# Eighteen more projection slices as seven products of halves in a hybrid mixer and MoE layer

## The reference

```python
proj = x @ w_in                       # 1024 -> 8 groups: lru_x, lru_y, ml_q, ml_k, ml_v, ml_o, gd_q, gd_k, gd_v, gd_z, gates
ha = rg_lru(causal_conv(lru_x), ...) * gelu(lru_y)                    # branch a
hb = rms_norm(mlstm_chunkwise(ml_q, ml_k, ml_v, ...)) * sigmoid(ml_o) # branch b
qkv = silu(causal_conv(concat(gd_q, gd_k, gd_v)))
hc = rms_norm(gated_delta_chunked(l2(q), l2(k), v, g, beta)) * silu(gd_z)  # branch c
merged = sum(sigmoid(gates[n]) * (h[n] @ w_br[n]) for n in range(3))
x = layer_norm(ALPHA * x + merged @ w_out)
x = layer_norm(ALPHA * x + moe(x))    # 32 experts, top 4, SwiGLU, d_ff 1024
```

## Time and profile before

| | us |
|---|---|
| median of three runs | 1292.63 (1292.39 to 1293.22) |
| profiled execution, its own time | 1292.72 |
| its span, first to last instruction | 1290.9 |
| PE busy in the span | 1247.0 (97%) |
| DVE busy | 375.3 (29%) |
| ACT busy | 163.7 (13%) |
| POOL busy | 103.3 (8%) |
| bytes moved | 463.06 MB, mean 359 GB/s |

### The profile page before, as it was taken

The page is one execution under the profiler, slowest core; times in us unless marked ns, Lnnn a source line. Parts: engine busy times, 40 slices in busy tenths (PEclk is TensorE's granted clock), DMA queues, the critical chain, the costliest instruction groups (busy, mean ns, idle before and its releaser), DMA issues.

```text
span 1290.9 us, 18843 instructions
## 1 busy us (share of the span) xinstructions
PE 1247.0 (97%) x8098; PEld 684.6 (53%) x8098; DVE 375.3 (29%) x821; ACT 163.7 (13%) x283; POOL 103.3 (8%) x89
## 2 busy tenths in 40 slices
PE   9999999999999999999999999999899999999896
PEld 8888889999864344344343443434243333434342
DVE  4857583553443120211202112121111112120213
ACT  1441621121030000000000000000000000000001
POOL 1000035644100000000000000000000000000001
PEclk9999999999999999999999999999999999999999
DMA  7645227357899999999999999999999999999995
GB/s 271 204 136 181 102 99 293 123 216 289 327 368 423 421 429 409 427 426 427 427 414 428 427 428 425 428 427 427 426 428 429 425 430 428 428 426 429 428 428 238
DMA packets 51180, 463.06 MB, mean 359 GB/s; under 512 B 11896, under 2 KB 13840, under 8 KB 17072
## 3 DMA queue, kind: packets, MB, share of 16 engines
q1 hardware_dynamic: 45280, 459.85, 86.6%
q10 hardware_dynamic: 5840, 2.32, 0.7%
HBM read 460.68 MB, written 1.47 MB: 358 GB/s over the span
## 4 chain that ended last, share of the span: by engine, by line
PE 68%; DMA 20%; issue 1%; POOL 0%; DVE 0%; ACT 0%; POOLq 0%; SPq 0%; DVEq 0%
PE ps L1164 26%; DMA mix<-expert_w 10%; PE ps L1182 10%; DMA ring<-expert_w 10%; PE ps L684 7%; PE ps L1061 4%; PE ps L1073 4%; PE ps L707 4%; PE ps L1157 3%; PE ps L984 2%; PE ps L718 1%; PE ps L1173 1%; PE ps L808 1%; PE ps L1191 1%; PE ps L937 0%
## 5 line engine op out<-in xcount | busy, mean ns | idle before, releaser
L1164 PE MATMUL ps<-ring,mix 128*64 128x512 f32 x1512 | 338.3, 592 | 0.1
L1164 PEld LDWEIGHTS ps<-ring,mix 128*64 128x64 f32 x1512 | 106.5, 137 | 194.8 <-issue 190.6
L1182 PE MATMUL ps<-ring,mix 128*64 128x512 f32 x752 | 170.1, 594 | 19.5 <-DMA ring<-expert_w 19.5
L707 PE MATMUL ps<-mix 128*128 128x256 f32 x736 | 162.1, 380 | 0.0
L707 PEld LDWEIGHTS ps<-mix 128*128 128x128 f32 x736 | 138.7, 190 | 19.7 <-issue 1.2
L2176 DVE TENSOR_SCALAR mix<-ps 128x512 f32<-128x512 f32 x32 | 22.1, 692 | 370.6 <-PE ps L1164 370.6
L1164 PE MATMUL ps<-mix 128*64 128x512 f32 x536 | 121.1, 593 | 3.9 <-DMA mix<-expert_w 3.7
L1182 PEld LDWEIGHTS ps<-ring,mix 128*64 128x64 f32 x752 | 53.0, 137 | 120.5 <-issue 98.0
L2185 DVE COPY mix<-ps 128x512 f32<-128x512 f32 x32 | 22.1, 692 | 240.6 <-PE ps L1173 240.6
L647 POOL TENSOR_TENSOR mix<-mix 128x1024 f32<-128x1024 f32 (+1 forms) x2 | 3.4, 1700 | 955.9 <-ACT mix L1592 955.9
L1164 PEld LDWEIGHTS ps<-mix 128*64 128x64 f32 x536 | 37.6, 137 | 77.0 <-issue 69.8
(11 more groups left out here) (294 smaller groups left out, 940.1 us busy)
## 6 DMA issues: line engine op xcount, KB each, us to landing
ring<-expert_w SPq DMA_DIRECT2D x121, 2048.0 KB, 30.7
mix<-expert_w SPq DMA_DIRECT2D x39, 2048.0 KB, 29.7
mix<-stream_w SPq DMA_DIRECT2D x42, 1024.0 KB, 4.9
ring<-expert_w SPq DMA_DIRECT2D x41, 1024.0 KB, 10.0
mix<-expert_w SPq DMA_DIRECT2D x22, 1024.0 KB, 21.8
mix<-stream_w SPq DMA_DIRECT2D x8, 512.0 KB, 4.2
mix<-first_w SPq DMA_DIRECT2D x4, 512.0 KB, 4.9
mix<-planes ACTq DMA_DIRECT2D x1, 1024.0 KB, 7.2
```

Source lines behind the costliest of these rows:

```text
L707: ins = mm(o[:, m * S:(m + 1) * S], w[:, c, m * P:(m + 1) * P], XT[c] if rhs is None else rhs[:, c, :], start=(m == 0 and c == 0), stop=(c ...
L1164: ins = mm(PS[64 * a:64 * a + 64, bank + g, :], XE[j][:, c, 64 * a:64 * a + 64], w[a][:, g * 512:g * 512 + 512], start=False, stop=(c == K ...
L1182: ins = mm(PS[64 * a:64 * a + 64, bank + h, :], HT[:, c // 4, c % 4, 64 * a:64 * a + 64], w[a][:, h * 512:h * 512 + 512], start=(c == 0), ...
```

## The change

`halved` now also holds for gz0, gz1 and for a new class `early`: lx, ly, mq, mk, mv, mo and gq2, gq3, which is 18 slices more. Each takes two PSUM banks. For gz, the result is put together by ACT and DVE as for the gates. For the 16 early slices it is put together by ACT and POOL: ACT copies the first bank into the slice's own tile and the second bank into one of two buffers `PB3` (`both_parts`), which waits for the finish of the slice two before; POOL's `finish` adds the pieces with eight additions of 128 columns and increments `combined`, and whoever read the slice waits for that. POOL's order is written out: sums run two slices ahead of the finish. For mv0 and mv1, which need tokens on the partitions, the operands of each product are exchanged. The sums of the branch input move from POOL to DVE (`branch_sums`). mo's sigmoid becomes an operation of its own behind the finish. DVE does `conv_lru(0)` behind the heads. The homes of `HAS` and `WS` move, so that expert place 5 is loaded earlier (after ga11) and the tail piece later.

```diff
 def halved(name):
-    return name[:2] == "ga" or name[:3] == "br0"
+    return name[:2] in ("ga", "gz") or name[:3] == "br0" or early(name)
+def early(name):
+    return name[:2] in ("lx", "ly", "mq", "mk", "mv", "mo") or name in ("gq2", "gq3")
...
-        HAS = [area(MIX, 112 + 2 * n, 512).rearrange("p (c n) -> p c n", n=P) for n in range(4)]
+        HAS = [area(RING, 88 + 2 * n, 512).rearrange("p (c n) -> p c n", n=P) for n in range(4)]
+        WS = [[area(MIX, 111 + 6 * k + 2 * n, 512).rearrange("p (c n) -> p c n", n=P) for n in range(3)] for k in range(2)]
+        PB3 = [area(MIX, 123 + 1.5 * n, 384).rearrange("p (q n) -> p q n", n=P) for n in range(2)]
+        PSUMS = area(MIX, 126, P)
...
                 if name == "ga11":
                     full(sp, closing("br03"))
-                    sp.dma_start(TAIL, expert_w[...]).then_inc(E("tail_in"), 16)
+                    sp.wait_ge(E("state"), NC)
+                    load_steps(5, 0, 5)
...
             full(sp, closing("ga23"))
-            load_steps(5, 0, 5)
+            sp.dma_start(TAIL, expert_w[...]).then_inc(E("tail_in"), 16)
...
+            def finish(name, dst):
+                i = early_at[name]
+                moved(gp, name + "a")
+                moved(gp, name + "b")
+                corners, middle = dst
+                b = PB3[i % 2]
+                nc_g.tensor_tensor(PSUMS, middle[0], middle[1], ALU.add)
+                nc_g.tensor_tensor(corners[1], corners[0], corners[1], ALU.add).then_inc(E("pool_own"), 1)
+                gp.wait_ge(E("pool_own"), 3 * i + 1)
+                for v in middle:
+                    ins = nc_g.tensor_tensor(v, v, corners[1], ALU.add)
+                ins.then_inc(E("pool_own"), 1)
+                gp.wait_ge(E("pool_own"), 3 * i + 2)
+                nc_g.tensor_tensor(corners[1], corners[1], PSUMS, ALU.add)
+                nc_g.tensor_tensor(corners[0], corners[0], b[:, 0, :], ALU.add)
+                for n, v in enumerate(middle):
+                    ins = nc_g.tensor_tensor(v, v, b[:, 1 + n, :], ALU.add)
+                ins.then_inc(E("pool_own"), 1)
+                gp.wait_ge(E("pool_own"), 3 * i + 3)
+                gp.sem_inc(E("combined"), 1)
...
+            weight_sums(at("gq2"))
+            weight_sums(at("gq3"))
+            finish("gq2", quarters(GIN[:, :, 3:], 2))
+            finish("gq3", quarters(GIN[:, :, 3:], 3))
+            weight_sums(at("lx0"))
+            weight_sums(at("lx1"))
+            for n in range(4):
+                weight_sums(at(f"lx{n + 2}" if n < 2 else f"ly{n - 2}"))
+                finish(f"lx{n}", quarters(LX[:, :, 3:], n))
             gp.wait_ge(E("gsilu_v"), 1)
             clear(X_, 0.0)
             clear(XTi, 0.0)
+            for n in range(4):
+                weight_sums(at(f"ly{n + 2}" if n < 2 else ("mq", "mk")[n - 2]))
+                finish(f"ly{n}", quarters(LY, n))
+            finish("mq", quarters(QM, 0))
+            weight_sums(at("mv0"))
+            finish("mk", quarters(MK, 0))
+            weight_sums(at("mv1"))
...
-            gp.wait_ge(E("ha_ready"), 1)
-            moving_sums(4, HAS, ...)
-            gp.wait_ge(E("mss"), 2 * NT)
-            for i in range(len(in_halves)):
+            for n in range(2):
+                weight_sums(at(f"mo{n}"))
+                finish(f"mv{n}", by_token(n))
+            for n in range(2):
+                weight_sums(at(f"gz{n}"))
+                finish(f"mo{n}", quarters(MO, n))
+            for i in range(at("ga00"), len(in_halves)):
                 weight_sums(i)
...
                     if made:
                         pe.wait_ge(E("weight_sums"), 4 * i + made)
+                    if name[:2] == "mv":
+                        lhs, rhs = rhs, lhs
...
+            def both_parts(name, dst, scale=1.0):
+                i = early_at[name]
+                full(act, name + "a")
...
+                nc_s.mul(dst, src, scale).then_inc(free(name + "a"), 1)
+                if i >= 2:
+                    act.wait_ge(E("combined"), i - 1)
+                full(act, name + "b")
+                nc_s.mul(PB3[i % 2].rearrange("p q n -> p (q n)"), ps(name + "b")[:, 0:3 * P], scale
+                         ).then_inc(free(name + "b"), 1)
...
             for n in range(6):
-                moved(dve, f"gq{n}")
+                if f"gq{n}" in early_at:
+                    dve.wait_ge(E("combined"), early_at[f"gq{n}"] + 1)
+                else:
+                    moved(dve, f"gq{n}")
...
             def gelu_argument():
-                for n in range(4):
-                    moved(dve, f"ly{n}")
+                dve.wait_ge(E("combined"), early_at["ly3"] + 1)
...
+            def branch_sums():
+                b11, b12, b21, b22 = [LY[:, 4 * k:4 * k + 4, t * P:(t + 1) * P] for k in range(2) for t in range(NT)]
+                for n, (dst, left, right) in enumerate(((HAS[0], b12, b11), (HAS[1], b22, HAS[0]), (HAS[2], b22, b12),
+                                                        (HAS[3], b21, HAS[1]))):
+                    tt(dst, left, right, ALU.subtract).then_inc(E("moving_sums"), 1)
+                    dve.wait_ge(E("moving_sums"), 4 + n + 1)
```

More of the change, by code:

```diff
@@ L234, in layer_kernel @@
     in_halves = [name for name, _, _ in stream if halved(name)]
+    early_at = {name: n for n, name in enumerate(name for name in in_halves if early(name))}
+    late_at = {name: n for n, name in enumerate(name for name in in_halves if not early(name))}
     def stream_value(n):
@@ L709, in proj @@
                                  start=(m == 0 and c == 0), stop=(c == nk - 1), skip_group_check=True)
[L710 to L719, removed]
                 done(name, ins)
@@ L826, in fill @@
                         if name == "ms00":
[L827 to L828 removed]
+                            pe.wait_ge(E("combined"), early_at["mk"] + 1)
                         t = int(name[3])
@@ L841, in fill @@
                         pe.wait_ge(E("ms_ready"), 1)
-                        for n in range(2):
-                            moved(pe, f"mv{n}")
+                        pe.wait_ge(E("combined"), early_at["mv1"] + 1)
                         for t in range(NT):
@@ L1437, in evac_v @@
             def evac_v(n):
-                full(act, f"mv{n}")
-                nc_s.copy(V1[:, :, 2 * n:2 * n + 2, 0:128],
-                          ps(f"mv{n}").rearrange("p (t h e) -> p t h e", t=NT, h=2)).then_inc(free(f"mv{n}"), 1)
+                both_parts(f"mv{n}", V1[:, :, 2 * n:2 * n + 2, 0:P].rearrange("p t h e -> p h t e"))
             act.wait_ge(E("gelu"), 2)
@@ L1450, in _ @@
             A(LU, LU, ACT.Sqrt).then_inc(E("lu"), 1)
-            evac("mo0", MO[:, 0:2, :], func=ACT.Sigmoid)
+            evac("mo0", MO[:, 0:2, :])
             for t in range(NT):
@@ L1460, in _ @@
                   scale=1.0 / MV).then_inc(E("mss"), 1)
-            evac("mo1", MO[:, 2:4, :], func=ACT.Sigmoid)
+            evac("mo1", MO[:, 2:4, :])
             for n in range(2):
[L1464 to L1467, removed]
+                act.wait_ge(E("combined"), early_at[f"mo{n}"] + 1)
+                A(MO[:, 2 * n:2 * n + 2, :], MO[:, 2 * n:2 * n + 2, :], ACT.Sigmoid).then_inc(E("zsig"), 1)
             def first_part(name, dst):
@@ L1472, in first_part @@
                 nc_s.copy(dst, ps(name + "a")).then_inc(E("part_copied"), 1)
+            for n in range(2):
+                first_part(f"gz{n}", GZ[:, 2 * n:2 * n + 2, :].rearrange("p c s -> p (c s)"))
+                moved(act, f"gz{n}b")
+                A(MT[n], GZ[:, 2 * n:2 * n + 2, :].rearrange("p c s -> p (c s)"), ACT.Sigmoid).then_inc(E("zsig"), 1)
+            gates = [f"{n}{d}" for kind, n, d in branch_items() if kind == "ga"]
             def gate(k):
@@ L1851, in mlstm_gate @@
             def mlstm_gate():
-                for n in range(2):
-                    moved(dve, f"mo{n}")
+                dve.wait_ge(E("zsig"), 2)
                 for h in range(MH):
@@ L1973, in o_gate @@
             def o_gate(t):
-                for n in range(2):
-                    moved(dve, f"gz{n}")
                 full(dve, f"ot{t}")
```

63 lines of the change are left out of this document (34 added, 29 removed).

## The result

The changed kernel takes 1362.83 us (median of 4 runs, 1361.23 to 1364.82), the kernel before 1292.93 (1292.39 to 1293.46): a ratio of 1.0541, 95% interval 1.0523 to 1.0560, or **+69.9 us**. The direction was forecast, the size was not: the sum said +34.3, and the result lies beyond the range. The profiled execution is the slowest of the four, 1364.82; its span is 1363.0.

What follows compares the result with a forecast made beforehand. PE's own work was taken to bound the first stage, full DMA engines the second, shifting as a block. Scores 38.3 us late less 4.0 given back made +34.3 on 1292.72, 1327.0; range 1297 to 1345.

Steps and rivals of the forecast that it cites:

- the sum: Whole kernel: scores 38.3 us late, less 4.0 given back by the last six slices, +34.3 us, 1327.0 in all.
- What is saved: PE: a slice in halves takes 6.25 us instead of 6.91; 18 slices by 0.66 are 11.9 us.
- POOL's additions: POOL's finish: an addition of 128 columns taken at 0.45 us, bounds 0.27 and 0.725; 4.0 us a slice with gaps.
- Is a SCALAR_TENSOR_TENSOR held?: DVE's convolutions: with both inputs in SBUF, one per POOL instruction, 1.41 us beside sums, about 0.6 beside a finish, instead of 0.49.
- Step 1: Rows stage: DVE's chain held beside POOL's sums of gq2 and gq3; scan at 34.0, gq4 at 37.2 instead of 33.9.
- Steps 2 to 5: Convolutions to scores: DVE held beside POOL; norms +9.7, at banks +24.7, inverse +37.4, y +35.4, scores +38.3 us.
- step 3: Decay arguments: convolution and other DVE ops beside POOL's sums and finishes; at banks taken by 121.8 instead of 97.1, +24.7.
- Step 6: After the scores: POOL has room, about 42 us of work in 58, and the last six slices give back 4.0 us.
- The edits costed at nothing: Branch sums on DVE, ACT's second copies, exchanged operands, place 5's load: taken as covered; +3 to +6 if the branch sums' cover goes.
- POOL alone: Rival: DVE hardly held, POOL's own work sets the pace to the scores; 1297 to 1315, chance 0.2.
- Faster: Rival: PE stays the pace if a finish takes 2.7 us and DVE isn't held; full gain 1280.8, chance 0.08.
- Worse than the sum: Rival: long DVE ops of 1024 and 2048 columns wait for POOL and hold it; +5 to +18, within main case's 0.69.

Runs made afterwards that it cites:

- before_adds: The kernel before with 24 and 36 additions of 512 columns on a spare tile added to POOL, nobody needing their results: 1314.41 us.
- before_sets: The kernel before with 30 and 45 memsets of 1024 columns on an unused area added to POOL: 1299.81 us.
- sets_full: The changed kernel with POOL's weight sums of gq2 to mv1 and finish additions of gq2 to mk replaced by memsets of about equal length: 1338.97 us.
- late_only: The changed kernel with only mv, mo and gz of the new slices in halves, gq2 to mk whole again: 1316.98 us.
- z_first: The changed kernel with gz0 put together ahead of the mLSTM's gate and ACT's sigmoid of gz0 ahead of mo's: 1348.15 us.
- z_mv1: z_first with POOL's finish(mv1) also moved ahead of mo1's weight sums: 1345.41 us.
- late_mended: late_only with gz0 put together before the mLSTM's gate and finish(mv1) ahead of mo1's sums: 1300.71 us.

## Why the prediction was right and wrong

- **What is saved** (0.66 a slice, 11.9 in all): right for a product at full clock (7.17 against 6.52 in the timeline), but outweighed, since PE now waits in slices 2 to 8 of the page and runs slower behind its waits. PE's busy time rose by 11.2 us (1247.0 to 1258.2) instead of falling by 11.9, while the mean granted clock fell from 0.998 to 0.976. No term of the prediction was for the clock.
- **POOL's additions**: right. The undisturbed ones of 128 columns take 0.41 to 0.46, where 0.45 was taken; the mean of 547 ns in the group above also has those that met DVE.
- **Is a SCALAR_TENSOR_TENSOR held?** Right, and shown by `before_adds` against `before_sets` and by `sets_full`.
- **Step 1** (scan ends at 34.0, gq4 at 37.2) was too small: they came at 39.3 and 42.7. What failed is "of some 20 ops only four and the reciprocal get through from 20.8 to 28". The seventeen ops on 8 columns ahead of the rows were left out. Undisturbed they take 0.17 to 0.20 each, 3.4 us in all, but beside POOL's sums they took from 17.97 to 29.05: about every second one is held for most of POOL's instruction, whatever its own size, 1.07 to 1.23 us each, and six in a row took 4.04 instead of 1.17. The ops on the rows themselves, which the step had as held, came behind POOL's sums and ran undisturbed.
- **Steps 2 to 5**: right in kind, with step 1's 5.5 us carried through to the norms (77.7 against 71.7). The at banks were taken at 122.7 (forecast 121.8), so step 3 was 5 us too long and made good step 1's error: that is luck. The inverse ended at 157.3 (153.2), y started at 172.2 (168.9), the scores at 177.6 (173.8). PE's waits stand where they were forecast, in front of gq4, for POOL's sums, before y for ACT, at the scores for POOL.
- **Step 6** is the step that failed: "After it POOL has room ..., and the last six slices give back 6 x 0.66 = 4.0". POOL does have room in the sum; it had none in the order of its queue. Instead of -4.0 the stretch from scores to u cost 26.0. Waits: 8.1 for finish(mv1), 13.3 for the bank and 0.9 at the transposes. Work at a lower clock: 2.9 for gz1, 2.7 for the numerators, 1.5 for mv0, 1.4 for the scores (2.93 against 1.58) and 0.3 in the solve. Against that stand 3.6 saved in the slices and a wait of 1.8 before the values that is gone; 0.3 are left over. `late_only` and `z_first` show the bank; for finish(mv1), `z_mv1` got 2.7 of the 8.1 back, and both mends together 16.3 of 24.0 in `late_mended`.
- **The edits costed at nothing** were the other face of it: "PE has two slices and the u and w products (15 us) before it needs br00" looked at who needs the branch sums, and not at what is queued behind them on DVE: the op that frees gz0's bank, which PE needs one slice later. The branch sums themselves are 2.9 us of that wait (248.6 to 251.4); before them DVE waits for ACT's sigmoid of mo until 242.0.
- **Rivals.** "POOL alone" fell as the mechanism of this kernel, yet `sets_full` shows it close behind. "Faster" fell. "Worse than the sum" held in sign, but its +5 to +18 were worked out from long DVE ops and not from the two waits, and are at most half of what came: +35.6 over the sum. The long ops did their part indirectly: beside them POOL's sums of mo0 took 9.18 instead of 5.3.
- **Open**: how much of the loss, early and late, is the clock's alone; no run was made with the waits kept and the clock at full. Nor does a run show how much of the 8.1 before the numerators could be had back with DVE's normalisation earlier.

## What to carry to other kernels

Where an engine holds another for the length of its own instruction, count the other's instructions and not only their time: here a chain of ops of 0.17 us lost the most for its length, 3.4 us that became 11.1. When work in a queue gets longer, list for every bank and buffer who frees it, and what now stands in front of that freeing op on its queue; room in the sum of an engine's time is no room in its order. A saving on the pacing engine is worth something only as long as it stays the pacing engine: here 0.66 us of PE a slice was paid with 9.4 us of POOL.

## What the runs showed of the hardware that was not expected

- A TENSOR_SCALAR with one SBUF input waits for a POOL memset (8 columns: 0.975 to 1.25 us instead of 0.17), while a SCALAR_TENSOR_TENSOR and a TENSOR_TENSOR with two SBUF inputs don't. In `sets_full`, timeline of DVE:

```profile
18.86 1.25 DVE L1687 TENSOR_SCALAR mix<-mix 128x8 f32<-128x8 f32 x1
...
20.39 0.17 DVE L1689 TENSOR_TENSOR mix<-mix 128x8 f32<-128x8 f32 x1
```

- Ops of 8 columns are held every second time: beside the eight sums of gq2 and gq3, 1.35 us each from start to start, held ones took 1.07 to 1.23 and those between them 0.17, while ops of 48 to 55 columns in the block inverse took 1.3 one after the other.
- The hold works in the other direction as well: four sums of POOL beside DVE's ops of 2048 columns took 9.18 us instead of 5.3.
- A wait of PE cost more than its length. The 56 matmul records of gz1 took 9.4 us after 13.3 us of idleness at a granted clock of 0.67, between the two levels of 1.2 and 2.4 GHz, 8.0 in `z_mv1` at 0.80, 6.5 in `z_first` at 1.00. Windows of gz1 in the changed kernel, in `z_mv1` and in `z_first`:

```profile
252.70:262.10 9.40, 9.40 (x58) 9.28 (x58) 2.19 (x5) 1.22 (x2) 0.00 (x0) 0.67 0.01 2
```

```profile
235.40:243.40 8.00, 7.99 (x58) 7.88 (x58) 6.12 (x7) 2.26 (x4) 5.78 (x6) 0.80 0.01 2
```

```profile
239.10:245.60 6.50, 6.46 (x58) 6.37 (x58) 4.50 (x5) 2.37 (x4) 6.02 (x8) 1.00 0.25 105
```
